# Two weight slots of the first expert item fetched into memory that the item leaves unused

## The chip, the cores and the metric

The kernel runs on one core of a Trainium2 chip. The metric is the device time of one execution in microseconds (us). Before the change three runs took 1303.74, 1305.22 and 1307.96 us; the median is 1305.22 us.

## The reference, cut to what matters

A two-layer decoder over 256 tokens of width 1024: differential attention, a dense SwiGLU, a second attention (MoBA), and then a mixture of 8 experts of which each token uses its top two. The change lies in the last part:

```python
def moe_swiglu(h, router, w_gate, w_up, w_down):
    B, S, D = h.shape
    tok = h.reshape(B * S, D)
    logits = (tok @ router).astype(jnp.float32)
    top_v, top_i = lax.top_k(logits, TOP_K_EXPERTS)
    w = jax.nn.softmax(top_v, axis=-1)
    gates = jnp.sum(jax.nn.one_hot(top_i, N_EXPERTS, dtype=jnp.float32) * w[..., None], axis=1)
    out = jnp.zeros_like(tok)
    for e in range(N_EXPERTS):
        out = out + gates[:, e:e + 1].astype(tok.dtype) * swiglu(tok, w_gate[e], w_up[e], w_down[e])
    return out.reshape(B, S, D)
```

Each expert has three float32 matrices of 1024 x 3584 (`D_EXPERT`), 44 MB together, 352 MB for the eight.

## The kernel before, in words

All large weights go through a ring of `RING` = 7 buffers of 2 MB (`ring0` to `ring6`, 16 KB in each of 128 partitions). A buffer's filling is a "slot". SyncE issues one DMA a slot, all on one queue (`load`, L576 to L579): it waits until the slot seven places earlier has been used, on the semaphore `group_used`, issues the DMA, and the DMA raises `slot_full[r]` when it has landed. A slot is `GS` = 8 groups of 128 x 512 values; TensorE raises `group_used` once for each group that it has multiplied.

The part before the experts (attention, the dense SwiGLU, attention) uses `NS` slots with `NG` groups. Its products are split: ScalarE copies a group into `whi`, rounded to fp32r, VectorE subtracts that from the raw group into `wlo`, and TensorE makes three products (L1571 to L1573: high x high, high x low, low x high). `whi` is a ring of 12 groups (24 KB per partition). Activations are split in the same way, into pairs such as `hhi`, `hlo`, `ihi`, `ilo` (4 KB per partition each, side by side in memory).

The experts are worked off as items, in an order that the routing finds. `KINDS` = "sbsbsbs" gives the first seven, and the loop from `LAST` on makes one more here, an "s". Each item reads all of one expert: 21 slots (`item_slots`), in the order gate, up (first column block), then for each pair of column blocks two gate slots, two up slots and one or two down slots, and four down slots at the end. All of an item's 21 slots are used in order.

- An "s" (few) item has up to 64 rows. TensorE multiplies the raw float32 weights straight from the ring (L1951, L1955 for gate and up, L1946 for down), 16 wide matmuls a slot. `whi`, `wlo` and the split activations stay unused.
- A "b" (big) item has up to 128 rows and splits its weights through `whi` and `wlo` as above, 24 matmuls a slot. ScalarE's `item_split` (L812) and VectorE's `item_halve` (L1436) do that. The first 8 groups of a big item are split at the end of the item before: on ScalarE in two halves with the copy `result` (L883) of the old item between them, on VectorE with the split of the second half of the item's rows (`gather_lo(i, 1)`, L1487) between group 6 and group 7.

In time: the last slot products of the second attention end, then comes the routing (logits, top two, ranks: short work on all engines), then item 0, item 1 and so on. Seven slots of item 0 are fetched before it begins, each when a buffer of the second attention comes free. Its eighth slot (`j` = 7) waits until its first slot has been used. SyncE's program is `item(0, 0)`, a wait for `table_set` (the expert numbers), then the items that follow.

`hhi`, `hlo`, `ihi` and `ilo` also hold the split residual for the router's logits (`T_part`); the last product that reads them raises `logit_mm`.

Of the kernel before, what the change touches and what calls it, by code (L numbers as in the profile page):

```python
# [22 lines left out]
F32 = mybir.dt.float32  # L23
# [7 lines left out]
P = 128  # L31
GROUP = 512
RING = 7
HL = 12
AHEAD = 8
LO_AHEAD = 6
GS = 8
SLOT = GS * GROUP
# [3 lines left out]
def trunk(nc, x, norm_mix, norm_ffn, diff_w_qkv, diff_w_o, diff_lambda, diff_subln, moba_w_qkv, moba_w_o,  # L42
# [54 lines left out]
    NS = len(slots)  # L97
    paired = [s for s in range(NS) if len(slots[s][0].shape) == 4]
    full_at = [16 * sum(2 if b in paired else 1 for b in range(s % RING, s + 1, RING)) for s in range(NS)]
    first_group = [sum(g for _, g in slots[:s]) for s in range(NS + 1)]  # L100
    NG = first_group[NS]
# [33 lines left out]
    item_slot = {key: j for j, key in enumerate(item_slots)}  # L135
    PAIRED = [(0, 1)] + [(c, 2) for c in range(1, NE, 2)]
    IS = len(item_slots)
    assert NE % 2
    IG = GS * IS
    KINDS = "sbsbsbs"  # L140
    LAST = len(KINDS)
    FEW = P // 2
    BIG_AT = [i for i in range(LAST) if KINDS[i] == "b"]
# [14 lines left out]
    with ExitStack() as ctx:  # L158
        def sb(name, shape, dt=F32, stack=ctx):
            return stack.enter_context(nc.sbuf_tensor(name, shape, dt))  # L160

        def sem(name):
            return ctx.enter_context(nc.semaphore(name))


        ring, wlo = [], []
        for slot in range(RING):
            raw = ExitStack()
            ring.append(sb(f"ring{slot}", [P, SLOT], F32, raw))
            raw.close()  # L170
            wlo.append(sb(f"wlo{slot}", [P, SLOT], F32R))
        whi = sb("whi", [P, HL, GROUP], F32R)
        expert_no = sb("expert_no", [P, E])
        items = ExitStack()
# [49 lines left out]
        attn.close()  # L224
        hidT = sb("hidT", [P, FBW, T])
        gain = hidT[:, :, :].rearrange("p b n -> p (b n)")
        hhi = sb("hhi", [P, FBW, T], F32R)
        hlo = sb("hlo", [P, FBW, T], F32R)
        ihi = sb("ihi", [P, KD, P], F32R)
# [65 lines left out]
        gain_in = sem("gain_in")  # L295
        router_in = sem("router_in")
        slot_full = [sem(f"slot_full{r}") for r in range(RING)]
        hi_done = sem("hi_done")
        lo_done = sem("lo_done")
        group_used = sem("group_used")  # L300
# [54 lines left out]
        logit_mm = sem("logit_mm")  # L355
# [80 lines left out]
        def part_of(t, s, g, size=1):  # L436
            slot = t[s % RING]
            if s in by_rows:
                k_blocks = slots[s][1] // 2
                half, k = half_and_k(s, g)  # L440
                return slot[:, 0:2 * k_blocks * GROUP].rearrange(
                    "p (k h n) -> p h k n", h=2, n=GROUP)[:, half, k:k + size, :]
            return slot[:, g * GROUP:(g + size) * GROUP].rearrange("p (g n) -> p g n", n=GROUP)

        def item_part(t, j, g, size):
            if j == IS - 1:
                half, k = divmod(g, FBW)
                return t[(NS + j) % RING][:, :].rearrange("p (k h n) -> p h k n", h=2, n=GROUP)[:, half, k:k + size, :]
            return part_of(t, NS + j, g, size)

        def hi_of(m, size):
            return whi[:, m % HL:m % HL + size, :]
# [10 lines left out]
        def n_items(eng):  # L463
            eng.wait_ge(table_set, 1)
            return eng.value_load(extra[0:1, 0:1], min_val=0, max_val=MAX_ITEMS - E) + E

        def slot_landed(i, j):
            last = max(s for s in range(NS) if s % RING == (NS + j) % RING)
            return i * (16 * IS // RING) + full_at[last] + 16 * (j // RING + 1)

        def used_at(i, m):
            return i * IG + (NG + m)
# [9 lines left out]

        def hi_free(i, m):
            if m < HL:
                return used_at(0, m + 2 - HL) if i == BIG_AT[0] else used_at(i - 2, IG + m + 2 - HL)
            return used_at(i, m + 2 - HL)

        def hlo_at(i, c):
# [57 lines left out]
        @block.sync  # L546
        def _(sp):
            for tb in range(TB):
                sp.dma_start(rowbuf[:, tb, :], x[0, tb * P:(tb + 1) * P, :]).then_inc(x_in[tb], 16)
            for s, (src, groups) in enumerate(slots):  # L550
                if s == 2:
                    sp.dma_start(lam, diff_lambda[0].partition_broadcast(P)).then_inc(lam_in, 16)
                    sp.dma_start(rt[:, :, :], moe_router[0].rearrange("(k p) e -> p k e", p=P)).then_inc(router_in, 16)
                if s >= RING:
                    sp.wait_ge(group_used, first_group[s - RING + 1])
                dst = ring[s % RING][:, 0:groups * GROUP]
                if s in paired:
                    dst = dst.rearrange("p (k a n) -> p k a n", a=2, n=T)
                    first = 0
                    if s == 0:  # L560
                        for j in range(3):
                            ks = slice(2 * j, 2 * j + 2)
                            for a in range(2):
                                sp.dma_start(dst[:, ks, a, :], src[:, ks, a, :]).then_inc(head_in[j], 16)
                        first = 6
                    for a in range(2):
                        sp.dma_start(dst[:, first:, a, :], src[:, first:, a, :]).then_inc(slot_full[s % RING], 16)
                else:
                    dst = dst.rearrange("p (k n) -> p k n", n=src.shape[2])
                    sp.dma_start(dst, src).then_inc(slot_full[s % RING], 16)  # L570


            used_past = sp.alloc_register("used_past")
            sp.reg_mov(used_past, NG + GS * (1 - RING))

            def load(r, dst, src):  # L576
                sp.wait_ge(group_used, used_past)
                sp.dma_start(dst, src).then_inc(slot_full[r], 16)
                sp.reg_add(used_past, used_past, GS)  # L579

            def item(i, e):
                for j, (kind, c, wide, part) in enumerate(item_slots):
                    r = (NS + j) % RING
                    if kind == "down":
                        src = moe_w_down[0][e, c * W:(c + 1) * W, :]
                        if few(i) and c == 0:
                            src = src.rearrange("(h p g) n -> p h (g n)", p=P, g=2)
                        else:
                            src = src.rearrange("(p g) n -> p (g n)", p=P)
                    else:  # L590
                        w, rows = moe_w_gate if kind == "gate" else moe_w_up, D // wide
                        src = w[0][e, part * rows:(part + 1) * rows, c * W:(c + wide) * W].rearrange("(k p) n -> p k n", p=P)
                    dst = ring[r][:, :]
                    if len(src.shape) == 3:
                        dst = dst.rearrange("p (k n) -> p k n", n=src.shape[2])
                    load(r, dst, src)

            item(0, 0)
            sp.wait_ge(table_set, 1)
            for i in range(1, LAST):  # L600
                e = sp.value_load(extra[0:1, 1 + i:2 + i], min_val=0, max_val=E - 1)
                item(i, e)
            n = n_items(sp)
            with sp.Fori(LAST, n) as i:
                e = sp.value_load(extra[0:1, bass.ds(i + 1, 1)], min_val=0, max_val=E - 1)
                item(i, e)

            for tb in range(TB):
                sp.wait_ge(out_first, tb + 1)
                sp.wait_ge(out_rows, tb + 1)  # L610
                sp.dma_start(out[0, tb * P:(tb + 1) * P, :], out_row(tb)).then_inc(stored, 16)
            sp.wait_ge(stored, 16 * TB)
# [3 lines left out]
        def _(act):  # L616
# [105 lines left out]
            for layer in range(2):  # L722
# [11 lines left out]
                for t in range(STEPS):  # L734
# [22 lines left out]
                    for s in ends[layer][t]:  # L757
                        kind, j = QKV[s - s0]
# [20 lines left out]
                for c in range(NF):  # L779
# [6 lines left out]
                    last = down_slot[c - 1] if 0 < c < NF - 1 else up_slot[c]  # L786
# [19 lines left out]
            def item_split(i, first, last):  # L806
                for m in range(first, last, 2):
                    j, g = m // GS, m % GS
                    if g == 0:
                        act.wait_ge(slot_full[(NS + j) % RING], slot_landed(i, j))  # L810
                    act.wait_ge(group_used, hi_free(i, m))
                    nc.scalar.copy(hi_of(NG + m, 2), item_part(ring, j, g, 2)).then_inc(hi_done, 2)  # L812

# [117 lines left out]
            n = n_items(act)  # L931
# [634 lines left out]
        def _(pe):  # L1566
# [355 lines left out]

            def few_products(i, j):
                kind, c, wide, part = item_slots[j]
                raw = ring[(NS + j) % RING]
                if kind == "gate" and c and part == 0:
                    pe.wait_ge(m_silu, i * NE + c)
                if kind == "down" and c == 0 and (not isinstance(i, int) or i):
                    pe.wait_ge(y_out, 2 * i)
                if kind == "down":  # L1930
                    pe.wait_ge(m_hhi, i * NE + (c + 1))
                pe.wait_ge(slot_full[(NS + j) % RING], slot_landed(i, j))
                for g in range(GS):
                    m = GS * j + g
                    if m in FEW_GATHER:
# [4 lines left out]
                    if kind == "down":  # L1940
                        k, half = g // 2, g % 2
# [11 lines left out]
                    else:  # L1953
                        ps, k, half = psA if kind == "gate" else psB, part * KD // 2 + g // 2, g % 2
# [103 lines left out]
```

## Time and profile before

| | |
|---|---|
| median of three runs | 1305.22 us |
| profiled execution | 1304.98 us, its span 1303.2 us |
| granted TensorE clock over the span | 0.99 |
| TensorE matmul busy | 95% of the span |
| DMA queue of the weights | 422.75 MB, 83.0% of 16 engines |
| chain that ended last | PE 79%, DMA 17%, DVE 2%, ACT 1% |

The span is that of the profiled execution; its own time is 1.8 us longer than the span and 0.24 us under the median. PE is TensorE's matmuls, PEld its weight loads, ACT ScalarE, DVE VectorE, POOL GpSimd, SPq the DMA issues of SyncE. A busy TensorE is not TensorE at its peak, since matmul ends are modelled. The granted clock is given as a share of 2.4 GHz; 0.50 is 1.2 GHz.

### The profile page before, as it was taken

Reading aid. Unit: us, or ns where it says so; the run is one execution under the profiler, and the core shown is the slowest. Engines: PE = TensorE matmul, PEld = TensorE weight load, DVE = VectorE, ACT = ScalarE, POOL = GpSimd, SP = SyncE. Lnnn points to the kernel's source line nnn. Section 1 sums busy time; section 2 is a strip of 40 time slices with the busy share of each in tenths; the row PEclk is TensorE's granted clock in tenths of the full one; section 3 lists DMA queues with packets and bytes.
Section 4 is the critical chain, followed back from the end, with each engine's and each line's share of the span. In section 5 each row is a group of like instructions: output and inputs, shape, how many; then the busy total and the mean of one; then the engine's idle time right before and its main releaser. Section 6 shows DMA issues by size and latency. Waiting matters only on the chain.

```text
span 1303.2 us, 18423 instructions
## 1 busy us (share of the span) xinstructions
PE 1242.6 (95%) x7254; PEld 880.2 (68%) x7254; DVE 637.7 (49%) x754; ACT 568.5 (44%) x871; POOL 112.3 (9%) x262
## 2 busy tenths in 40 slices
PE   9999999999999999899999989999989999998776
PEld 8988999999989833577853367774338777333222
DVE  6886755547755300588820078880028885000001
ACT  6665544435656300577720177761027775001002
POOL 1000000000000461100210100201010021001000
PEclk9999999999999899999999999999999999999999
DMA  9943554358432399999999999999999999999996
GB/s 332 356 152 115 184 195 162 130 174 279 171 143 78 129 401 418 404 415 415 408 369 415 417 408 415 421 383 391 416 409 412 414 416 359 417 419 402 415 416 256
DMA packets 116487, 424.47 MB, mean 326 GB/s; under 512 B 4625, under 2 KB 23218, under 8 KB 108594
## 3 DMA queue, kind: packets, MB, share of 16 engines
q1 hardware_dynamic: 116192, 422.75, 83.0%
q8 instruction: 58, 0.95, 0.3%
q10 hardware_dynamic: 210, 0.54, 0.1%
q14 instruction: 27, 0.22, 0.0%
HBM read 422.23 MB, written 1.05 MB: 325 GB/s over the span
## 4 chain that ended last, share of the span: by engine, by line
PE 79%; DMA 17%; DVE 2%; ACT 1%; issue 1%; SPq 0%; POOL 0%; POOLq 0%; ACTq 0%; DVEq 0%
DMA ring<-in_moe_w_down 8%; PE psA L1571 7%; PE psA L1573 7%; PE psA L1572 7%; PE psB L1571 7%; PE psB L1573 7%; PE psB L1572 7%; DMA ring<-in_moe_w_up 6%; PE psA L1955 5%; PE psB L1955 5%; PE psY L1571 5%; PE psY L1573 5%; PE psY L1572 5%; PE psY L1946 4%; DMA ring<-in_moe_w_gate 2%; PE psY L1719 1%
## 5 line engine op out<-in xcount | busy, mean ns | idle before, releaser
L1436 DVE TENSOR_TENSOR wlo<-ring,whi 128x2048 fp32r<-128x2048 f32 (+1 forms) x135 | 287.2, 2150 | 84.9 <-ACT whi L812 83.9
L812 ACT CAST whi<-ring 128x1024 fp32r<-128x1024 f32 x252 | 261.0, 1051 | 89.1 <-PE psA L1573 28.6
L1183 DVE TENSOR_TENSOR wlo<-ring,whi 128x1024 fp32r<-128x1024 f32 (+2 forms) x104 | 152.3, 1485 | 17.8 <-ACT whi L630 17.7
L630 ACT CAST whi<-ring 128x1024 fp32r<-128x1024 f32 (+1 forms) x134 | 133.4, 1023 | 59.3 <-PE psY L1573 28.2
L1946 PE MATMUL psY<-ring,squares_of 128*64 128x512 f32 x560 | 126.8, 596 | 7.3 <-DMA ring<-in_moe_w_down 7.1
L1515 DVE TENSOR_TENSOR hidT<-psB,hidT 128x512 f32<-128x512 f32 (+1 forms) x16 | 10.0, 625 | 243.4 <-PE psB L1955 177.4
L1955 PE MATMUL psB<-ring,resT 128*64 128x512 f32 x480 | 106.6, 594 | 8.9 <-DMA ring<-in_moe_w_up 8.8
L1955 PE MATMUL psA<-ring,resT 128*64 128x512 f32 x480 | 107.6, 596 | 5.6 <-DMA ring<-in_moe_w_gate 5.6
L1571 PE MATMUL psA<-xhi,whi 128*128 128x256 f32 x368 | 104.9, 285 | 2.6 <-DVE wlo L1183 1.2
L1571 PE MATMUL psB<-xhi,whi 128*128 128x256 f32 x368 | 106.4, 289 | 0.0
L1572 PE MATMUL psA<-xlo,whi 128*128 128x256 f32 x368 | 102.8, 279 | 0.0
L1572 PE MATMUL psB<-xlo,whi 128*128 128x256 f32 x368 | 102.7, 279 | 0.0
L1573 PE MATMUL psB<-xhi,wlo 128*128 128x256 f32 x368 | 102.6, 279 | 0.0
L1573 PE MATMUL psA<-xhi,wlo 128*128 128x256 f32 x368 | 102.6, 279 | 0.0
L839 ACT COPY squares_of<-psB 128x512 f32<-128x512 f32 (+1 forms) x20 | 10.6, 532 | 209.9 <-PE psB L1920 209.9
L1946 PEld LDWEIGHTS psY<-ring,squares_of 128*64 128x64 f32 x560 | 40.6, 137 | 82.2 <-issue 81.5
L1955 PEld LDWEIGHTS psB<-ring,resT 128*64 128x64 f32 x480 | 33.9, 137 | 79.5 <-issue 64.5
L1571 PE MATMUL psA<-whi,ihi 128*128 128x512 f32 x168 | 69.7, 415 | 15.4 <-DVE wlo L1436 15.4
L1955 PEld LDWEIGHTS psA<-ring,resT 128*64 128x64 f32 x480 | 33.0, 137 | 71.5 <-issue 63.2
L1571 PEld LDWEIGHTS psA<-xhi,whi 128*128 128x128 f32 x368 | 69.2, 188 | 4.5 <-issue 3.3
L1571 PEld LDWEIGHTS psB<-xhi,whi 128*128 128x128 f32 x368 | 69.4, 189 | 0.0
L1572 PEld LDWEIGHTS psB<-xlo,whi 128*128 128x128 f32 x368 | 69.3, 188 | 0.0
(351 smaller groups left out, 2265.0 us busy)
## 6 DMA issues: line engine op xcount, KB each, us to landing
ring<-in_moe_w_gate SPq DMA_DIRECT2D x56, 2048.0 KB, 19.0
ring<-in_moe_w_up SPq DMA_DIRECT2D x56, 2048.0 KB, 20.4
ring<-in_moe_w_down SPq DMA_DIRECT2D x56, 2048.0 KB, 21.0
ring<-in_ffn_w_gate SPq DMA_DIRECT2D x5, 2048.0 KB, 9.1
ring<-in_ffn_w_up SPq DMA_DIRECT2D x5, 2048.0 KB, 7.9
ring<-in_ffn_w_down SPq DMA_DIRECT2D x5, 2048.0 KB, 8.0
ring<-in_moba_w_qkv SPq DMA_DIRECT2D x8, 1024.0 KB, 7.4
ring<-in_diff_w_qkv SPq DMA_DIRECT2D x6, 1024.0 KB, 12.2
```

The lines of the kernel that those rows point to most:

```text
L630: nc.scalar.copy(hi_of(m, size), part_of(ring, s, g, size)).then_inc(hi_done, size)
L812: nc.scalar.copy(hi_of(NG + m, 2), item_part(ring, j, g, 2)).then_inc(hi_done, 2)
L839: nc.scalar.copy(few_hid[:, n % 2, 0:2 * wide, :], psB[:, 1, 0:wide * FEW_HALF].rearrange("p (b t) -> p b t", t=P)).then_inc(m_hhi, wide)
L1183: nc.vector.tensor_tensor(part_of(wlo, s, g, size), part_of(ring, s, g, size), f(hi_of(m, size)), ALU.subtract).then_inc(lo_done, size)
L1436: nc.vector.tensor_tensor(item_part(wlo, j, g, step), item_part(ring, j, g, step), f(hi_of(NG + m, step)), ALU.subtract).then_inc(lo_done, ...
L1515: nc.vector.tensor_tensor(act_, up_, act_, ALU.mult).then_inc(m_hid, wide)
L1571: mm(ps, xh, wh, start=start, stop=False, skip_group_check=shared)
L1572: mm(ps, xh, wl, start=False, stop=False, skip_group_check=shared)
L1573: return mm(ps, xl, wh, start=False, stop=stop, skip_group_check=shared)
L1719: ins = mm(psY[:, 3, i * wide:(i + 1) * wide], probsT[:, u % 2, i * (tb + 1) + kb, :], val[:, kb, c:c + wide], start=kb == 0, stop=kb == tb)
L1946: ins = mm(psY[half * FEW:(half + 1) * FEW, 0, :], x, at, start=c == 0 and k == 0, stop=c == NE - 1 and k == FBW - 1)
L1955: ins = mm(ps[half * FEW:(half + 1) * FEW, 0, :], few_in[:, k, :], at, start=k == 0, stop=k == KD - 1)
```

## The change

In item 0, slots `j` = 7 and `j` = 8 no longer go into the ring. Slot 7 goes into `ahead0`, which lies over the first 16 of `whi`'s 24 KB; slot 8 into `ahead1`, which lies over `hhi`, `hlo`, `ihi` and `ilo`. Slot 7 waits until all groups before the experts have been used (`group_used` >= `NG`), slot 8 until the logits' last product (`logit_mm` >= 1). Each has a semaphore of its own. The slots behind them take the ring places in order, so slot `j` = 9 of item 0 goes where slot 7 went and waits for what slot 7 waited for (item 0's first slot used). Slot 16 reuses the buffer of slot 9 and waits for that one. The ring place of every slot of later items is counted anew (`SHIFT` = 19 instead of 21 slots of item 0 in the ring), and their waits are as before: seven slots back. The first big item's first 12 `whi` groups now wait until item 0's slot 7 has been used.

```diff
+    AHEAD_SLOTS = 2
+    SHIFT = IS - AHEAD_SLOTS
...
+        early = ExitStack()
+        ahead = [sb("ahead0", [P, SLOT], F32, early)]
+        early.close()
         whi = sb("whi", [P, HL, GROUP], F32R)
...
+        early = ExitStack()
+        ahead.append(sb("ahead1", [P, SLOT], F32, early))
+        early.close()
         hhi = sb("hhi", [P, FBW, T], F32R)
...
+        def is_ahead(i, j):
+            return isinstance(i, int) and i == 0 and RING <= j < RING + AHEAD_SLOTS
+
+        def ring_at(i, j):
+            if not isinstance(i, int) or i:
+                return (NS + SHIFT + j) % RING
+            return (NS + (j if j < RING else j - AHEAD_SLOTS)) % RING
...
         def hi_free(i, m):
             if m < HL:
-                return used_at(0, m + 2 - HL) if i == BIG_AT[0] else used_at(i - 2, IG + m + 2 - HL)
+                return used_at(0, GS * (RING + 1)) if i == BIG_AT[0] else used_at(i - 2, IG + m + 2 - HL)
             return used_at(i, m + 2 - HL)
...
-            def load(r, dst, src):
+            def load(i, j, dst, src):
+                if is_ahead(i, j):
+                    sp.dma_start(dst, src).then_inc(ahead_full[j - RING], 16)
+                    return
                 sp.wait_ge(group_used, used_past)
-                sp.dma_start(dst, src).then_inc(slot_full[r], 16)
+                sp.dma_start(dst, src).then_inc(slot_full[ring_at(i, j)], 16)
                 sp.reg_add(used_past, used_past, GS)
 
             def item(i, e):
                 for j, (kind, c, wide, part) in enumerate(item_slots):
-                    r = (NS + j) % RING
+                    first = isinstance(i, int) and i == 0
+                    if first and j == RING:
+                        sp.wait_ge(group_used, NG)
+                    if first and j == RING + 1:
+                        sp.wait_ge(logit_mm, 1)
+                    if first and j == 2 * RING + AHEAD_SLOTS:
+                        sp.reg_add(used_past, used_past, GS * AHEAD_SLOTS)
...
             def few_products(i, j):
                 kind, c, wide, part = item_slots[j]
-                raw = ring[(NS + j) % RING]
+                raw = ahead[j - RING] if is_ahead(i, j) else ring[ring_at(i, j)]
...
-                pe.wait_ge(slot_full[(NS + j) % RING], slot_landed(i, j))
+                if is_ahead(i, j):
+                    pe.wait_ge(ahead_full[j - RING], 16)
+                else:
+                    pe.wait_ge(slot_full[ring_at(i, j)], slot_landed(i, j))
```

`slot_landed`, `item_part` and ScalarE's `item_split` follow the new ring places.

## Rows read from the trace of the kernel before

**Rows 1.** The page's span in 40 equal slices: DMA share in tenths.

```profile
DMA  9943554358432399999999999999999999999996
```

**Rows 2.** Windows: stretch, its length, engines busy (instructions), PEclk, DMA share, GB/s.

```profile
445.00:450.00 5.00, 5.00 (x26) 4.99 (x26) 0.00 (x0) 1.58 (x8) 4.00 (x14) 0.50 0.01 3
450.00:455.00 5.00, 5.00 (x31) 2.91 (x32) 0.16 (x1) 0.28 (x2) 4.22 (x21) 0.61 0.00 0
...
500.00:540.00 40.00, 33.86 (x173) 14.12 (x172) 4.55 (x7) 8.93 (x16) 9.48 (x16) 0.99 1.02 413
540.00:640.00 100.00, 100.00 (x432) 79.28 (x432) 86.75 (x56) 76.45 (x81) 7.31 (x7) 0.99 1.02 414
...
660.00:680.00 20.00, 20.00 (x126) 11.98 (x126) 2.07 (x2) 3.58 (x12) 3.88 (x5) 1.00 0.92 342
```

**Rows 3.** Timeline of SyncE's issues: start, us, instruction, count in the row.

```profile
436.93 0.37 SPq L578 DMA_DIRECT2D ring<-in_moe_w_down  x1
455.63 3.82 SPq L578 DMA_DIRECT2D ring<-in_moe_w_gate  x2
```

**Rows 4.** Chain of waits: the router's logits (start, us, what).

```profile
438.35 1.11 PE psA L1828 x8
```

**Rows 5.** Slot 0 of item 1: its issue, and the time to its landing.

```profile
L578 SPq DMA_DIRECT2D ring<-in_moe_w_gate x1: 403/403/403, 508.0 to 508.0; - x1
...
DMA to landing us min/median/max: 27.2/27.2/27.2
```

**Rows 6.** Slots 4 and 5 of item 2: issues, and time to landing.

```profile
L578 SPq DMA_DIRECT2D ring<-in_moe_w_up x2: 372/372/373, 652.8 to 660.9; - x2
...
DMA to landing us min/median/max: 7.6/8.6/9.6
```

**Rows 7.** Timeline of TensorE over items 0, 1, 2 (start, us, instruction, [idle <-releaser]).

```profile
515.17 3.65 PE L1946 MATMUL psY<-ring,squares_of 128*64 128x512 f32 x16 [0.50 <-DMA ring<-in_moe_w_down]
...
527.55 7.09 PE L1946 MATMUL psY<-ring,squares_of 128*64 128x512 f32 x32
539.67 0.79 PE L1571 MATMUL psA<-whi,ihi 128*128 128x512 f32 x1 [5.03 <-DVE wlo L1436]
...
543.93 0.40 PE L1571 MATMUL psA<-whi,ihi 128*128 128x512 f32 x1
...
546.73 0.40 PE L1571 MATMUL psB<-whi,ihi 128*128 128x512 f32 x1
...
666.87 1.51 PE L1951 MATMUL psA<-ring,resT 128*64 128x256 f32 x11
```

**Rows 8.** Timelines of ScalarE and VectorE between item 0 and item 1.

```profile
527.66 1.14 ACT L824 ACTIVATE ihi<-psY,gain_cols 128x128 fp32r<-128x128 f32 x4 [4.43 <-PE psY L1883]
535.23 1.99 ACT L812 CAST whi<-ring 128x1024 fp32r<-128x1024 f32 x2 [6.43 <-issue]
537.13 0.58 ACT L883 COPY resT<-psY 128x512 f32<-128x512 f32 x1
...
537.32 3.43 DVE L1436 TENSOR_TENSOR wlo<-ring,whi 128x2048 fp32r<-128x2048 f32 x2 [12.93 <-ACT whi L812]
540.67 1.12 DVE L1487 SCALAR_TENSOR_TENSOR ilo<-psY,gain_cols,ihi 128x128 fp32r<-128x128 f32 x4
```

**Rows 9.** Windows of 1 us, TensorE alone: matmul busy, granted clock, DMA.

```profile
538.00:539.00 1.00, 0.00 (x0) 1.00 1.05 393
...
541.00:542.00 1.00, 1.00 (x4) 0.50 1.01 406
```

**Rows 10.** Timeline of TensorE where item 5 begins.

```profile
973.98 0.80 PE L1571 MATMUL psA<-whi,ihi 128*128 128x512 f32 x1 [5.33 <-DVE wlo L1436]
...
978.84 0.63 PE L1573 MATMUL psA<-whi,ilo 128*128 128x512 f32 x1
```

**Rows 11.** Groups by shape, ScalarE: busy us, mean ns.

```profile
L812 ACT CAST whi<-ring 128x1024 fp32r<-128x1024 f32 x252 | 261.0, 1051 | 89.1 <-PE psA L1573 28.6 <-issue 22.7 <-PE psB L1573 21.9
L630 ACT CAST whi<-ring 128x1024 fp32r<-128x1024 f32 x126 | 128.8, 1047 | 59.3 <-PE psY L1573 28.2 <-PE psB L1573 18.6 <-PE psA L1573 10.2
```

More of the change, by code:

```diff
@@ L297, in trunk @@
         slot_full = [sem(f"slot_full{r}") for r in range(RING)]
+        ahead_full = [sem(f"ahead_full{a}") for a in range(AHEAD_SLOTS)]
         hi_done = sem("hi_done")
@@ L447, in item_part @@
                 half, k = divmod(g, FBW)
-                return t[(NS + j) % RING][:, :].rearrange("p (k h n) -> p h k n", h=2, n=GROUP)[:, half, k:k + size, :]
-            return part_of(t, NS + j, g, size)
+                return t[(NS + SHIFT + j) % RING][:, :].rearrange("p (k h n) -> p h k n", h=2, n=GROUP)[:, half, k:k + size, :]
+            return part_of(t, NS + SHIFT + j, g, size)
         def hi_of(m, size):
@@ L465, in n_items @@
             return eng.value_load(extra[0:1, 0:1], min_val=0, max_val=MAX_ITEMS - E) + E
-        def slot_landed(i, j):
-            last = max(s for s in range(NS) if s % RING == (NS + j) % RING)
-            return i * (16 * IS // RING) + full_at[last] + 16 * (j // RING + 1)
+        def is_ahead(i, j):
[4 more added lines that the diff above has]
+            return (NS + (j if j < RING else j - AHEAD_SLOTS)) % RING
+        def slot_landed(i, j):
+            r = ring_at(i, j)
+            last = max(s for s in range(NS) if s % RING == r)
+            if isinstance(i, int) and i == 0:
+                return full_at[last] + 16 * ((j if j < RING else j - AHEAD_SLOTS) // RING + 1)
+            in_first = sum(1 for n in range(SHIFT) if (NS + n) % RING == r)
+            return (i - 1) * (16 * IS // RING) + full_at[last] + 16 * (in_first + j // RING + 1)
         def used_at(i, m):
@@ L592, in item @@
                         src = w[0][e, part * rows:(part + 1) * rows, c * W:(c + wide) * W].rearrange("(k p) n -> p k n", p=P)
-                    dst = ring[r][:, :]
+                    dst = (ahead[j - RING] if is_ahead(i, j) else ring[ring_at(i, j)])[:, :]
                     if len(src.shape) == 3:
                         dst = dst.rearrange("p (k n) -> p k n", n=src.shape[2])
-                    load(r, dst, src)
+                    load(i, j, dst, src)
             item(0, 0)
@@ L809, in item_split @@
                     if g == 0:
-                        act.wait_ge(slot_full[(NS + j) % RING], slot_landed(i, j))
+                        act.wait_ge(slot_full[ring_at(i, j)], slot_landed(i, j))
                     act.wait_ge(group_used, hi_free(i, m))
```

## Prediction

> **What bounds the kernel now.** I read the slices of the span first. From the fifteenth slice on (a slice is 32.6 us, so from about 456 us) the DMA share stays at nine tenths or more almost to the end, while the slices before it lie at two to eight [rows 1]. The expert part is therefore bound by the weights' transfers, or close to it, and the question is when this stream begins and whether it ever stands still. The windows answer both. Its begin: the seventh slot of item 0 is issued at 436.93 us, the next only at 455.63 us [rows 3], and from 445 to 455 us the DMA engines move nothing (shares 0.01 and 0.00) [rows 2]. Its stops: the share falls to 0.92 at 660 to 680 us, where item 1 (big) gives way to item 2 (few) [rows 2], and there the time from issue to landing is down to 7.6 us [rows 6] against 27.2 us at the start of item 1 [rows 5]. A transfer that is alone in the queue can't be much faster than 7.6 us: 2.10 MB at 413 GB/s [rows 2] is 5.1 us, and the rest is fixed. So at the end of item 1 the queue is empty, and the transfers wait for TensorE to free ring buffers.
>
> The two bounds take turns. In a few item a slot of 16 matmuls takes 7.09/2 = 3.5 us of TensorE [rows 7], less than the 5.1 us of its transfer: TensorE catches up, and the landings set the pace. In a big item it takes longer: from 546.73 us (slot 1 begins) to 666.87 us (item 2 begins) are 20 slots, 6.0 us each with the turns and scatters between them [rows 7]: TensorE sets the pace, and the transfers run ahead until the ring is full. TensorE has no gap in that stretch (busy 100.00 of 100 us) [rows 2].
>
> **What the change moves.** Slots 7 and 8 of item 0 no longer wait for item 0's first slot. Slot 7's new wait is that of slot 6 (all groups used), so it goes out at about 437.3 us, right behind it [rows 3]. Slot 8 waits for the logits' last product, which ends at 438.35 + 1.11 = 439.5 us [rows 4]. On SyncE only item 0's slot 9 and what follows is queued behind that wait, and it can't go before 455.63 us anyway, 16 us of slack. Slot 6 lands at 436.93 + 7.7 = 444.6 us, an estimate from the 7.6 us of [rows 6]; slots 7 and 8 land 5.1 us apart, at about 449.7 and 454.8 us, in the idle stretch. Slot 9 then takes slot 7's old issue time, 455.63 us, and each slot of item 0 behind it has the landing that the slot two before it had. The stream runs 2 x 5.1 = 10.2 us ahead. Behind slot 8, slots 9 to 15 may be nine slots ahead of TensorE; from slot 16 on it is seven again, and slots that TensorE frees at 3.5 us each are issued faster than 5.1 us each, so the queue doesn't run dry within item 0.
>
> TensorE's waits on the stream are what this can save. In item 0 it is 0.50 us before slot 17 [rows 7]; the gaps of the turns and gathers stay. So item 0 ends 0.5 us sooner, at 534.64 - 0.5 = 534.1 us (527.55 + 7.09 [rows 7]).
>
> The large one stands between item 0 and item 1: 5.03 us in which TensorE waits for `wlo` [rows 7]. Behind that stands the landing of item 1's slot 0 at 508.0 + 27.2 = 535.2 us [rows 5]: ScalarE begins to round at 535.23 us, after 6.43 us without work, VectorE ends its first piece at about 539.6 us (2.3 us from 537.32) [rows 8]. With the stream 10.2 us ahead this slot lands at 525.0 us, before ScalarE has finished the gathered rows at 527.66 + 1.14 = 528.8 us [rows 8]. That is what is late next. Step by step, each duration from [rows 8]: `whi` of groups 0 to 3 until 528.8 + 2.0 = 530.8; their `wlo` until 533.1. TensorE ends item 0 at 534.1 and goes on at once. ScalarE then copies the result (0.6 us, to about 534.8) and rounds groups 4 to 7 until 536.8; VectorE subtracts groups 4 and 5 (1.15 us) until 537.0, splits the second half of the rows (1.1 us, the first of its four columns at 537.3, all at 538.1), subtracts 6 and 7 until 539.25. TensorE needs 0.70 us a group at full clock ((546.73 - 543.93) / 4 [rows 7]): groups 0 to 3 until 536.9, then a wait to 537.4; groups 4 and 5 until 538.8, a wait to 539.3; 6 and 7 until 540.7. In the kernel before slot 1 begins at 546.73 us [rows 7]. So **item 1's second slot begins 6.0 us sooner**: 0.5 of item 0, 5.0 of the gap, 1.4 of a clock that need not fall (next paragraph), less 0.9 of new small waits.
>
> The clock: before, it is still 1.00 at 538 us and 0.50 at 541 us, after 5.03 us of idle [rows 7, 9]; slot 0 took 546.73 - 539.67 = 7.06 us instead of 8 x 0.70 = 5.6, so 1.4 us were lost. The waits left over are about 0.5 us each. I take no fall there. The Trainium skill, "TensorE: Matmul & The Clock Gate", section "HAM oscillation — how this bites in real kernels", says that waiting on DMA lets the gate halve the clock and that the next stretch of matmuls starts slow; the trace agrees at this place. By it the sum would be the one above.
>
> From here on item 1 is paced by TensorE, so its end moves from 666.87 to 660.9 us. The stream, 10.2 us ahead, is now 4.2 us further ahead of TensorE than it was, but the last issue of item 1's phase already finds an empty queue (7.6 us) and the one before it is 2.0 us from that [rows 6]: these 4.2 us turn into idle DMA time, a few transfers earlier than now. Where item 2 begins, issues and landings follow TensorE in both kernels, 6.0 us sooner. Everything behind (item 5 begins with a wait of 5.33 us [rows 10]; the DMA share stays at nine tenths to the last slice [rows 1]) is the same work shifted.
>
> What else is added costs nothing on the path: two waits and a register add on SyncE, which has slack; TensorE waits on another semaphore for slots that landed before item 0 began to free buffers; `hi_free` of item 1 asks for item 0's slot 7, used before slot 17 begins at 515.17 us [rows 7]. Two transfers now run beside the routing. Bound of that cost: the same cast takes 1051 ns in the expert part, with the DMA engines full, and 1047 ns before it, with them under half busy [rows 1, 11]: 0.4%, under 0.1 us of the 18.7 us of routing. I take 0. The Trainium skill, "DMA: Bandwidth & Descriptors", section "Queues, rings and completion order", says that each DMA engine serves its queues in turn, packet by packet; instruction fetches would then wait behind weights where they now find idle engines. No row separates that out for the routing, and the sum doesn't include it.
>
> **Sum.** 1304.98 us (profiled execution, 0.24 under the median) - 6.0 = 1299.0; against the median 1305.22 it is 1299.2. I forecast 1299.1 us.
>
> Bounds: the handover can keep more of its wait. If the clock does fall in it, 1.4 us come back (item 1's loss), up to 2.6 us (item 5: twelve matmuls from 973.98 to 978.84 + 0.43 us at half clock, 5.3 us, of which half is lost [rows 10]). The phases in which items 3 and 5 begin also shift by 6 us; item 5 lost 2.6 us to its slow stretch and item 1 1.4, so these may give or take 1 us each. That makes 1297 to 1302.
>
> **The rivals.**
> 1. *The whole lead survives.* If no ring-full phase took it back, the end would move by 10.2 us: 1295.0. For it: the DMA share of 1.02 through item 1 [rows 2]. Against: the empty queue at 660.9 us [rows 6]. Chance 0.04.
> 2. *The handover stays late.* Item 1 starts through a chain on ScalarE and VectorE that the landing hides today. If the result copy or the second half of the rows holds TensorE longer, and the clock falls, 3 to 4 us of the 6 are gone: 1302 to 1303.5. For it: the first 8 groups depend on work after item 0's last matmul. Against: only half of them do. Chance 0.17. That it doesn't do what it says (slot 7 or 8 not issued until 455 us) gives 1305: 0.04.
> 3. *Slower: the routing suffers.* Transfers beside it hold up instruction fetches or short operations between 437 and 455.6 us. All of that stretch is on the path, and what it loses is lost at the end. It decides once the loss is over 6.0 us, a third of the stretch; at 10 us the time is 1309. Against: 0.4% on the cast [rows 11]. Chance 0.04.
>
> **How the numbers follow.** Forecast (4 to 8 us saved) 0.71, rival 1 0.04, rival 2 0.17 and no effect 0.04, slower 0.04. 0.3% of 1305 us is 3.9 us, about what a measurement tells from no change: the time must be under 1301.3. Of the forecast's case and rival 1 nearly all is below it, of rival 2 hardly any: faster 0.73, same 0.24, slower 0.03. For the range I take 1296.6 to 1303.3: it leaves out rival 1, no effect, the slower case and small ends of the others, some 0.17.
>
> **What would show it.** Slots 7 and 8 issued at about 437 and 440 us, DMA share near 1 from 445 to 455 us; TensorE's start of item 0 unmoved; landing of item 1's slot 0 at 525 us; the first matmul of item 1 near 534.2 us with gaps of about 0.5 us behind it and clock 1.00; item 2 beginning near 660.9 us; a larger dip of the DMA share before that; the same 6 us at items 3 and 5. The step most likely to be wrong is the handover; if item 2 begins less than 4 us sooner, it failed there. If item 2 begins 6 us sooner and the end doesn't, the items behind lose it again, through the clock.

## The result and the profile after

The changed kernel took 1293.88 us (median of 7 runs, 1291.82 to 1296.77), the kernel before 1305.43 us (7 runs, 1300.12 to 1307.96): a ratio of 0.9919, 95% interval 0.9898 to 0.9940. I had forecast 1299.1 us and a range of 1296.6 to 1303.3. The change is faster, as forecast, but by 11.6 us instead of 6, and the time lies below the range. The profiled execution took 1293.82 us.

The page's slices of the kernel after (granted clock and DMA share in tenths), against [rows 1]:

```profile
PEclk9999999999999999999999989999999999999999
DMA  9943554349333699999999999999999999999995
```

The stream begins within the fourteenth slice instead of at its end. Windows of the kernel after, with the columns of [rows 2]:

```profile
440.00:445.00 5.00, 4.30 (x35) 4.05 (x36) 2.81 (x12) 2.98 (x10) 2.03 (x6) 1.00 1.00 417
445.00:450.00 5.00, 5.00 (x48) 4.06 (x49) 0.16 (x1) 1.85 (x8) 3.96 (x14) 1.00 1.04 419
450.00:455.00 5.00, 5.00 (x46) 3.08 (x44) 0.48 (x1) 0.47 (x1) 4.20 (x22) 1.00 1.01 405
...
540.00:640.00 100.00, 100.00 (x440) 79.38 (x439) 87.98 (x53) 76.14 (x81) 7.31 (x7) 1.00 1.02 412
...
645.00:655.00 10.00, 10.00 (x46) 7.85 (x44) 4.55 (x2) 3.83 (x10) 3.77 (x5) 1.00 0.79 298
```

Two columns differ from [rows 2] in 445 to 455 us. The DMA share is 1.04 and 1.01 where it was 0.01 and 0.00: that is the change. But the granted clock (third from the right) is 1.00 and 1.00 where it was 0.50 and 0.61, and TensorE has 48 and 46 matmuls there instead of 26 and 31. I had not expected that, and it is not obviously the change's doing.

SyncE's issues, and TensorE where items 0, 1 and 2 begin (columns as in [rows 3, 7]):

```profile
436.98 0.37 SPq L602 DMA_DIRECT2D ring<-in_moe_w_down  x1
437.45 2.45 SPq L599 DMA_DIRECT2D ahead<-in_moe_w_gate  x2
450.78 3.82 SPq L602 DMA_DIRECT2D ring<-in_moe_w_up  x2
```

```profile
447.07 3.67 PE L1984 MATMUL psA<-ring,resT 128*64 128x256 f32 x32
450.57 1.68 PE L1984 MATMUL psB<-ring,resT 128*64 128x256 f32 x14
...
509.65 3.60 PE L1979 MATMUL psY<-ring,squares_of 128*64 128x512 f32 x16
...
521.13 7.09 PE L1979 MATMUL psY<-ring,squares_of 128*64 128x512 f32 x32
528.14 0.50 PE L1601 MATMUL psA<-whi,ihi 128*128 128x512 f32 x1
...
531.58 0.48 PE L1601 MATMUL psA<-whi,ihi 128*128 128x512 f32 x1 [0.37 <-DVE ilo L1517]
...
533.40 0.50 PE L1601 MATMUL psA<-whi,ihi 128*128 128x512 f32 x1 [0.18 <-DVE wlo L1466]
...
534.91 0.40 PE L1601 MATMUL psB<-whi,ihi 128*128 128x512 f32 x1
...
655.04 1.30 PE L1984 MATMUL psA<-ring,resT 128*64 128x256 f32 x10
```

The wait of 5.03 us before item 1 has gone: the first product with `whi` follows item 0's last slot at once, and waits of 0.37 and 0.18 us are left in its slot 0. Item 1's second slot begins at 534.91 us, 11.8 us sooner than in [rows 7]. Item 2 begins 11.8 us sooner (655.04), and the span ends 11.2 us sooner.

Where do 11.8 us come from, when I expected 6.0? Item 0's second slot (the first on `psB`) begins at 450.57 us here; in the kernel before it was this:

```profile
449.99 5.60 PE L1951 MATMUL psA<-ring,resT 128*64 128x256 f32 x32
455.42 2.76 PE L1951 MATMUL psB<-ring,resT 128*64 128x256 f32 x24
```

455.42 - 450.57 = 4.85 us are gained before item 0's second slot, under the same work: the routing's matmuls and item 0's slot 0 ran at half clock before and at full clock after. From there to item 1's second slot it is 84.34 us after and 91.31 us before. So this pair of profiles says: 4.85 us of clock and 6.97 us of what I had forecast as 6.0. Is the 4.85 us luck, or the change's?

### The profile page after: what moved, and what is told of

It is laid out like the page before. It is cut to its first block, busy times and chain, and to the rows that moved or that the text cites. A ratio compares the mean times of both kernels' runs of the same rounds, so it can differ in the third digit from the quotient of the medians.

```text
span 1292.0 us, 18420 instructions
## 1 busy us (share of the span) xinstructions
PE 1236.0 (96%) x7254; PEld 875.0 (68%) x7254; DVE 638.3 (49%) x754; ACT 568.1 (44%) x871; POOL 112.1 (9%) x262
## 4 chain that ended last, share of the span: by engine, by line
PE 81%; DMA 13%; DVE 2%; ACT 1%; issue 1%; SPq 1%; POOL 0%; POOLq 0%; ACTq 0%; DVEq 0%
PE psA L1601 7%; DMA ring<-in_moe_w_down 7%; PE psB L1601 7%; PE psB L1603 7%; PE psA L1603 7%; PE psB L1602 7%; PE psA L1602 7%; PE psA L1988 6%; PE psB L1988 6%; PE psY L1979 5%; PE psY L1601 5%; PE psY L1603 5%; PE psY L1602 5%; DMA ring<-in_moe_w_up 4%; DMA ring<-in_moe_w_gate 2%; PE psY L1749 1%
## 5 line engine op out<-in xcount | busy, mean ns | idle before, releaser
L1988 PE MATMUL psA<-ring,resT 128*64 128x512 f32 x448 | 100.6, 596 | 5.6 <-DMA ring<-in_moe_w_gate 5.6
L1601 PE MATMUL psA<-whi,ihi 128*128 128x512 f32 x168 | 69.3, 413 | 10.6 <-DVE wlo L1466 10.3
```

The lines of the kernel that those rows point to most:

```text
L1601: mm(ps, xh, wh, start=start, stop=False, skip_group_check=shared)
L1988: ins = mm(ps[half * FEW:(half + 1) * FEW, 0, :], few_in[:, k, :], at, start=k == 0, stop=k == KD - 1)
```

## The experiments

The lines of the traces shift with each kernel's edits; the instructions are the same. Differences between few runs are read with care here: the kernel before alone spreads from 1299.2 to 1309.5 us.

**The same two kernels again.** No edit, more runs and a second profile of each.

> The kernel before, once more, for a second look at the clock of the routing stretch (437 to 456 us). In its first profile the granted clock was 0.50 from 443.69 to 453.93 us, and the matmuls of that stretch took 4.9 us longer than in the changed kernel's profile, where it was 1.00. Chance theory: up to 444 us both kernels do the same at the same times, so whether the clock falls there is drawn anew in each execution: runs of this kernel fall into two groups about 4.9 us apart, near 1300 and near 1305 us, and those of the changed kernel too. Rival theory, the change itself keeps the clock up: this kernel lies near 1305 us in all runs, clock 0.50 in the routing each time.

> The changed kernel, once more. Chance theory: the change is worth 7.0 us (item 1's second slot begins 11.8 us sooner in its profile, of which 4.85 us are the routing's clock), plus or minus 1 to 2 us for the slow stretches at the starts of items 1, 3 and 5; so the runs lie near 1292 us with full clock in the routing and near 1297 us without. Rival theory, the change keeps the clock up: all runs lie within 2 us of 1292 and each profile shows clock 1.00 from 437 to 456 us.

Measured: the kernel before 1302.48 us (12 runs), and 1305.06 us in 29 more beside these experiments; the changed kernel 1297.34 us (7 runs; ratio to the 29 runs 0.9932, interval 0.9902 to 0.9961).

The runs do lie in two groups. Of the 48 runs of the kernel before up to here (7 of the result, 12, 29), 20 lie below 1303 us (mean 1300.8) and 28 above 1303.7 (mean 1306.0). Of 14 runs of the changed kernel, 7 lie from 1290.7 to 1293.9 us (mean 1292.4) and 7 from 1296.0 to 1298.6 us (mean 1297.2). The changed kernel has the higher group too, so it doesn't keep the clock up: the rival falls. Group against group the change is worth 8.4 and 8.8 us, over all runs 1303.8 - 1294.8 = 9.0 us. In the seven runs each of the result, six of the kernel before were in its higher group and three of the changed kernel: by an estimate, 3/7 x 4.85 = 2.1 us of the 11.6 are that draw. So the 7.0 us of the second expectation is less than the runs give.

4.85 us, as a price of one draw, is an estimate: the second profile of the kernel before, an execution of 1302.93 us and so in the lower group, still loses time in the routing. From the start of the logits' last eight products (438.35 us in [rows 4]) to item 0's second slot the kernel before takes 17.07 us in its first profile and 15.46 in its second, the changed kernel 12.18 and 12.17: 4.9 and 3.3 us lost, and nothing.

The mean granted clock of each run goes with the groups: 0.991 in the lower and 0.988 in the higher group of 41 runs of the kernel before (12 and 29), 0.993 and 0.990 in those of the changed kernel. No run of the changed kernel's higher group was profiled; that its routing is what is slow there is shown by the half-lead version below, whose profile has it, and by the experiment with the clock held.

The windows of the routing in the second profiles (columns as in [rows 2]), first the kernel before, then the changed one:

```profile
443.00:454.00 11.00, 11.00 (x72) 8.51 (x73) 0.59 (x2) 2.34 (x9) 9.06 (x37) 0.69 0.01 4
```

```profile
443.00:454.00 11.00, 11.00 (x99) 8.24 (x100) 1.15 (x3) 2.33 (x9) 9.06 (x37) 1.00 1.02 411
```

The first profile of the kernel before had 0.53 in this window, this one 0.69: half clock for 2 x 0.47 x 11 = 10.3 us there and for 2 x 0.31 x 11 = 6.8 us here, in the same kernel. From item 0's second slot to item 1's second slot the kernel before takes 91.42 us here (544.41 - 452.99), the changed one 84.32 (534.14 - 449.82): 7.1 us.

**The traffic without the lead.** Both early fetches are made, and nothing reads them; the ring works as before.

```diff
+                    if isinstance(i, int) and i == 0 and j == RING:
+                        for a, spare_slot in enumerate((spare0, spare1)):
+                            sp.wait_ge(*((group_used, NG), (logit_mm, 1))[a])
...
+                            sp.dma_start(spare_slot[:, :].rearrange("p (k n) -> p k n", n=2 * W), more).then_inc(spare_full[a], 16)
```

> The kernel before with two more transfers of 2 MB: slots 7 and 8 of item 0 are fetched into the unused memory with the new kernel's waits, and then fetched again through the ring as before; nothing reads the early copies. So the traffic beside the routing is there and the lead of the stream is not. Theory of the lead (all of the gain is the earlier landing of item 1's first slot): no gain, 1305 us, within 1 us of the kernel before for the same clock in the routing; item 1 begins about 5 us after the end of item 0's matmuls. Rival theory, the traffic (or full DMA engines) keeps the clock of the routing up: 1.00 from 437 to 456 us, and about 1300 us in all runs. Rival theory, traffic hurts the routing: TensorE begins item 0 later than 450.0 us with the same clock.

Measured: 1304.20 us (12 runs), ratio 0.9993, interval 0.9975 to 1.0012. No gain and no loss. The window of the routing, TensorE's start of item 0 and of item 1:

```profile
443.00:455.00 12.00, 11.86 (x63) 9.52 (x64) 1.61 (x4) 2.04 (x9) 9.81 (x39) 0.57 0.94 382
```

```profile
449.51 6.30 PE L1967 MATMUL psA<-ring,resT 128*64 128x256 f32 x32
...
539.87 0.53 PE L1587 MATMUL psA<-whi,ihi 128*128 128x512 f32 x1 [5.06 <-DVE wlo L1452]
```

DMA engines at 0.94 and a clock of 0.57 in the same window: full DMA engines don't keep the clock up. Item 0 begins at 449.51 us (449.99 before), so they don't hold up the routing either, which was my slower rival; the Trainium skill, "SBUF — State Buffer", section "SBUF: two separate sides", says that DMA traffic and the engines reach the memory by separate ports and can't contend, and the trace agrees. The clean comparison, at full clock, comes from two kernels further down, with the clock held: from the start of the logits' last eight products to item 0's second slot it is 12.11 us without the early transfers and 12.11 us with them. Item 1 begins after the old wait, 5.06 us: the gain is the lead and not the traffic.

**Half the lead.** `AHEAD_SLOTS` = 1, so that only slot 7 is fetched ahead:

```diff
-    AHEAD_SLOTS = 2
+    AHEAD_SLOTS = 1
```

> Only slot 7 is fetched ahead, into the rounded weights' memory; slot 8 goes through the ring. The stream's lead is 5.1 us, or less with full clock in the routing, instead of 10.2. Theory of the handover: what counts is that item 1's slot 0 has landed when TensorE ends item 0. With 5.1 us it lands at 530.0 us, its four first groups are split by 534.3 us, TensorE ends item 0 at 533.5 us: nearly all is gained, 6 of the 7 us; 1299 us with the slow clock in the routing and 1294 to 1295 us without. Rival theory, the gain goes with the lead: half of it, 3.5 us, 1302 us and 1297 us.

Measured: 1297.76 us (11 runs, 1293.41 to 1303.42), ratio 0.9949, interval 0.9928 to 0.9971. The runs don't fall into two clean groups, so the median alone decides little. The profile does for the start of item 1:

```profile
535.08 0.50 PE L1601 MATMUL psA<-whi,ihi 128*128 128x512 f32 x1 [1.75 <-DVE wlo L1466]
```

From item 0's second slot to item 1's second slot it takes 540.78 - 455.69 = 85.09 us. So 6.2 of the 7.0 us are there with half the lead. The granted clock of this profile is 0.57 from 443 to 454 us: an early fetch doesn't keep the routing at full clock. But over all runs the mean is 1298.1 us against 1294.8: 3.3 us apart, more than the 0.75 of the profile. The open part was whether that is the clock; the last experiment asks it.

**The clock held in both kernels.** TensorE gets transposes whose results nobody reads, in two small gaps of the routing and where it waits for the first split weights. The cut shows the kernel before; in the changed kernel the last condition is `if i in (3, 5)`, since it no longer waits at item 1.

```diff
             pe.wait_ge(count_set, 1)
+            keep_clock(4, psY[:, 3, :])
...
             pe.wait_ge(rows_set, 1)
+            keep_clock(5, psY[:, 3, :])
...
             def expert(i):
+                if i in (1, 3, 5):
+                    keep_clock(34)
```

> The kernel before with idle work for TensorE so that its clock need not fall: 4 and 5 transposes in the two small gaps of the routing, and 34 transposes (4.1 us) at the start of items 1, 3 and 5, where it waits 5 us for the first split weights. Clock theory: the runs of the kernel before fall into two groups (about 1301 and 1306 us) by the routing's clock, and each of the three items loses 1.4 to 3.4 us in a slow stretch. With the clock held all runs lie in one group, 1300.8 less some 6 us: 1294 to 1296 us, and the profile shows 1.00 from 437 us to the start of item 7. Rival theory: the two groups have another cause, then the spread stays and the time falls by 0 to 2 us. Item 1 still begins after a wait for its slot 0: the stream's lag isn't touched.

> The changed kernel with the same idle work in the routing and at the start of items 3 and 5 (not item 1, where it no longer waits). Against the kernel before with the clock held this gives the change's worth with no clock in it. Theory: 5.03 us of wait gone, 1.6 us in item 0, less 1.0 us of new small waits, 5.6 us; so 1288 to 1290 us, all runs in one group. Rival theory, the clock is no part of the gain: 8 to 9 us between the two kernels as between the two groups of the plain kernels.

> The changed kernel with the 4 and 5 transposes in the routing alone. Theory: the higher of its two groups (1297 us) goes, all runs lie near the lower one, 1292.5 us. Rival theory: so little added work doesn't hold the clock, and the two groups stay; or it delays the routing by more than 0.5 us.

Measured, 4 runs each: the kernel before with the clock held 1294.89 us (1294.43 to 1295.72; ratio to the plain kernel before 0.9920, interval 0.9895 to 0.9946); the changed kernel with the clock held 1288.45 us (1287.83 to 1289.96; 0.9874, 0.9847 to 0.9900); the changed kernel with the routing's transposes alone 1291.48 us (1291.16 to 1291.80; 0.9895, 0.9870 to 0.9920). The spread of 8 to 10 us has shrunk to 0.6 to 2.1 us, and each expectation on the clock held. Windows of the routing and of the start of item 3, first of the kernel before with the clock held, then of the changed kernel with the routing's transposes alone:

```profile
443.00:454.00 11.00, 11.00 (x98) 7.96 (x99) 0.79 (x3) 2.33 (x9) 9.06 (x38) 1.00 0.31 99
...
744.00:751.00 7.00, 5.80 (x44) 4.62 (x41) 3.29 (x2) 4.37 (x5) 0.00 (x0) 1.00 1.05 396
```

```profile
443.00:454.00 11.00, 11.00 (x100) 8.39 (x101) 1.14 (x4) 2.33 (x9) 8.98 (x36) 1.00 1.02 410
740.00:748.00 8.00, 4.47 (x12) 3.55 (x13) 6.81 (x9) 6.50 (x8) 0.00 (x0) 0.57 1.04 403
```

In the second the routing is at 1.00 and the start of item 3 still at 0.57, and that kernel is 3.0 us above the one with the clock held in items 3 and 5 too. Two such starts, so about 1.5 us each by this pair. The kernel before gives (1303.8 - 1294.9 - 28/48 x 4.85) / 3 = 2.0 us each, an estimate that is too high if the lower group loses something in the routing too. Item by item the profiles say: in the three without held clock and without lead, slot 0 of items 1, 3 and 5 takes 7.00 to 7.25, 7.25 to 8.30 and 7.16 to 8.25 us, and 5.70 with the clock held. So item 1's start is the cheapest of the three; from item 0's second slot to item 1's second slot these profiles take 91.31 to 91.47 us, 1.1 to 1.3 us more than with the clock held.

With no clock in it the change is worth 1294.89 - 1288.45 = 6.4 us. My expectation said 5.6; the rival (8 to 9 us, as between the plain kernels) falls. In the profiles, from item 0's second to item 1's second slot: 539.61 - 449.43 = 90.18 us before, 534.81 - 450.47 = 84.34 after, 5.8 us. The other 0.6 us of the medians has no place that can be shown. From item 2's begin to item 3's second slot it is 95.98 us against 94.92 in this pair, but that stretch varies by more than this without a change: from item 2's begin to item 3's first product it is 91.1 and 89.2 us in the two profiles of the changed kernel, and 89.1 us in the kernel that has the traffic and no lead.

With the clock of item 1's start (1.1 to 1.3 us) the plain change should then be worth 7.5 to 7.7 us, by an estimate; the groups of the plain kernels say 8.4 and 8.8. The last 1 us between them stays open.

TensorE around the start of item 1 in the kernel before with the clock held: the wait for the landing stands there all the same, filled with transposes.

```profile
521.81 7.09 PE L1947 MATMUL psY<-ring,squares_of 128*64 128x512 f32 x32
528.83 3.93 PE L1726 MATMUL psB<-ident 128*128 128x128 f32 x34
533.91 0.49 PE L1571 MATMUL psA<-whi,ihi 128*128 128x512 f32 x1 [1.16 <-DVE wlo L1436]
```

**What is left at the start of item 1.** The changed kernel with the clock held, and ScalarE splits all 8 groups before the result copy:

```diff
+                early = AHEAD if first else AHEAD // 2
                 if not few(i + 1):
-                    item_split(i + 1, 0, AHEAD // 2)
+                    item_split(i + 1, 0, early)
                 result(i)
                 if not few(i + 1):
-                    item_split(i + 1, AHEAD // 2, AHEAD)
+                    item_split(i + 1, early, AHEAD)
```

> As the changed kernel with the clock held, and ScalarE splits all of item 1's first 8 groups before the result copy of item 0, in the 4 us in which it has no work there. Theory: the small waits of 0.37 and 0.18 us in item 1's slot 0, and the latencies beside them, go; 0.8 us less than the version without. Rival theory: the result copy, now behind four more casts, or VectorE's order holds TensorE longer: no gain or a loss up to 1 us.

Measured: 1286.53 us (1285.92 to 1287.70), ratio to the kernel before 0.9859, interval 0.9834 to 0.9885; 1.9 us less than without. The timeline of ScalarE, then of TensorE:

```profile
521.28 3.89 ACT L842 CAST whi<-ring 128x1024 fp32r<-128x1024 f32 x4
527.35 0.59 ACT L913 COPY resT<-psY 128x512 f32<-128x512 f32 x1 [2.17 <-PE psY L1981]
```

```profile
527.17 0.49 PE L1602 MATMUL psA<-whi,ihi 128*128 128x512 f32 x1
...
532.88 0.40 PE L1602 MATMUL psB<-whi,ihi 128*128 128x512 f32 x1
```

Slot 0 of item 1 takes 5.71 us instead of 534.81 - 528.04 = 6.77: 1.06 us, the waits and what stood beside them. The expectation was 0.8; of the other 0.9 us in the medians (4 runs each) I don't know the place. This version is faster than both kernels.

**Half the lead, clock held.** As the changed kernel with the clock held, `AHEAD_SLOTS` = 1.

> One slot ahead instead of two, with the clock held as in the changed kernel with the clock held (routing, items 3 and 5). It separates the lead from the clock: one slot ahead gave 1298.1 us on average over its runs and two slots 1294.8, while the profile shows only 0.75 us between them up to item 1's second slot. Theory of the handover: half the lead gives all but 0.8 to 1.5 us; 1289.5 to 1290 us against 1288.45 and 1294.89 us; the rest of the 3.3 us was the clock. Rival theory, the gain goes with the lead: half of the 6.4 us, 1291.7 us. A slow stretch can still come at item 1's start, where TensorE waits 1.7 us: then 1 to 3 us more in some runs.

Measured: 1289.72 us (four runs, 1288.79, 1288.89, 1290.54 and 1292.14). The median is 1.3 us above two slots ahead and 5.2 below none. But the three were not measured side by side: the kernel before took 1304.35 us beside this version and 1305.99 us beside the other two (7 runs each). As ratios to the kernel before the three are 0.9887 (0.9861 to 0.9913) with one slot ahead, 0.9874 with two and 0.9920 with none. So of the whole gain half the lead brings between about a half and four fifths, and the rival's 1291.7 us, which supposed the same kernel before, can't be excluded. What the profile shows is the handover, the start of item 1:

```profile
529.75 0.51 PE L1601 MATMUL psA<-whi,ihi 128*128 128x512 f32 x1 [1.39 <-DVE wlo L1466]
```

From item 0's second slot to item 1's second slot it takes 535.46 - 450.72 = 84.74 us, against 84.34 with two slots and 90.18 with none: 5.4 of the 5.8 us at this place. There the theory of the handover holds and a gain in step with the lead doesn't.

Whether the 3.3 us between the means of the plain kernels were the clock is not settled. In the profiled run, the longest of the four, item 3's second slot comes 97.72 us after item 2's begin, against 94.92 with two slots. From item 2's begin to item 3's first product both kernels with one slot are long, 92.0 us here and 91.6 without held clock, against 88.9 to 91.1 in the five profiles with two slots and 89.1 to 90.5 in the four with none. Two profiles don't tell a cause from chance here, and it stays open.

## Why the prediction was right and where it failed

- *The stream begins in the idle stretch and runs 10.2 us ahead.* Right but for the size of the lead, 9.1 us (next point): issues at 437.45 us and right behind, the DMA share 1.00 to 1.04 from 440 to 455 us. That slots 7 and 8 cost the routing nothing was right too (the traffic alone: ratio 0.9993).
- *Item 1's slot 0 lands before ScalarE wants it, and the handover is what is late next.* Right in mechanism. The landing came at 503.2 + 18.1 = 521.3 us, 13.9 us sooner; 4.85 of them are the routing's clock, so the lead was 9.1 us where I had 10.2. ScalarE took it up when the gathered rows were done. The new waits were 0.37 and 0.18 us with the restarts beside them, slot 0 took 6.77 us; my steps gave 6.6.
- *Item 0 ends 0.5 us sooner.* Wrong size: from item 0's slot 1 to its slot 19 it is 527.55 - 455.42 = 72.13 us before and 521.13 - 450.57 = 70.56 after, 1.6 us. The pair with the clock held gives 1.8 us (521.81 - 449.43 = 72.38 and 521.02 - 450.47 = 70.55). The trace before had this row, in which the wait of 0.62 us is put down to "issue":

```profile
520.03 1.24 PE L1883 MATMUL psY<-pick,normed 128*128 128x128 f32 x9 [0.62 <-issue]
```

The gather stands in the program behind the wait for slot 18, which landed at 496.4 + 23.6 = 520.0 us. So it was a wait for the stream, and it went with the 0.50 us before slot 17; I had left it standing with "the gaps of the turns and gathers stay".

- *The lead beyond TensorE's gain is lost at the end of item 1.* Right, as far as the traces can tell. From item 1's second slot to item 2's begin it is 120.13 to 120.17 us in all eleven profiles, whatever the lead: TensorE alone paces this stretch. The lead turns into idle DMA time at its end: the DMA share is 0.95 from 652 to 672 us before and 0.88 from 640 to 660 us after, each from 15 us ahead of item 2, and the fetches issued from 641 to 650 us land within 7.6 to 8.4 us, as from an empty queue. Whether a little of the lead comes through to item 3 is not shown.
- *The clock: 1.4 us regained at item 1, no fall.* Right: there is none, and three profiles without the lead lost 7.00 to 7.25 us less 5.70, that is 1.3 to 1.6 us, in that slot; 1.1 to 1.3 us of it reach item 1's second slot.
- *The failed step is the sum's base.* "1304.98 us (profiled execution, 0.24 under the median) - 6.0" starts from one execution whose routing ran at half clock, and took that for a property of the kernel. The clock columns of [rows 2] (0.50 and 0.61) stood in my own rows, beside the DMA share that I read there. That the routing can run at full clock was no term of the sum and had no place in the range. In the first two profiles it is 4.85 us. The second, smaller failure is item 0, 1.6 us instead of 0.5. Up to item 1's second slot that is the whole account: 6.0 + 1.1 - 0.1 = 7.0 us, and with 4.85 the 11.8 us that were measured.
- *What was luck.* Which runs of seven have the slow routing is a draw. The changed kernel's next seven runs had a median of 1297.34 us, inside my range, with the same code. For the medians of the result, the draw is 2.1 us by the estimate above, and the change itself 7.5 to 8.8 us; that leaves 0.7 to 2.0 of the 11.6 us without an account, within the interval of the ratio (0.9898 to 0.9940, which is 7.8 to 13.3 us).
- *The rivals.* The whole lead (10.2 us, 1295.0) comes closest to the measured number and was still wrong as a mechanism: with half the lead 5.4 of 5.8 us are there at item 1, and the 120.1 us of item 1 don't shrink with any lead. The late handover and the slower routing didn't happen.

## What to carry to other kernels

Before a sum is made against a profiled execution, read its granted clock over each stretch on the path: a stretch at half clock that other runs don't have is a term of the range, and a reason to compare more than a few runs. A lead in a stream is worth first of all the waits that it removes, here the landing on which the next item's first split weights stand; half the buffers brought 5.4 of the 5.8 us there, and the stretch behind it, which TensorE paces, took the same 120.1 us with any lead. What the whole run keeps of the second buffer is between a fifth and a half of the gain, and not settled. And a few matmuls of no use in a wait that TensorE has anyway were worth as much as the change: together with an earlier split the kernel goes from 1305 to 1286.5 us.

## What the runs showed of the hardware

- The clock of the routing stretch differs from execution to execution under work that is the same up to there (6.16 us of TensorE's matmuls between 436 and 443 us in the first profile of each kernel): 0.50 for 10.3 and for 6.8 us in the two profiles of the kernel before, 1.00 in both of the changed kernel, and a mean of 0.57 over 443 to 454 us in the kernel with one slot ahead. The Trainium skill, "TensorE: Matmul & The Clock Gate", section "What's actually happening", says that the point where the clock changes depends on where the work falls in the gate's own timing and so varies from run to run; the 10.3 and 6.8 us of one kernel agree.
- Nine transposes in gaps of 0.26 and 0.39 us were enough to keep it at 1.00 in the profiles of all five kernels that have them, and the runs of each came within 0.6 to 3.4 us of one another.
- Two transfers of 2 MB beside the routing, at a DMA share near 1, cost it nothing that shows: 12.11 us from the logits' last eight products to item 0's second slot with them and without, both at full clock.
